# Gated linear attention as masked score blocks instead of a carried state, with a new order of the work around it

## The chip, the core and the metric

The kernel runs on one core of a Trainium2 chip. The engines named below are TensorE (PE, the matrix engine; PEld is its weight load), VectorE (DVE), ScalarE (ACT), GpSimd (POOL) and SyncE (SP, which here only starts DMAs). Each takes its own instructions in order, and they wait for each other through semaphores. The metric is the device time of one execution in microseconds (us), the median of several runs.

## What is computed

Two decoder layers over 272 tokens (16 meta tokens and 256 of the sequence), width 1024. Each layer is a half-step SwiGLU FFN, a mixer and a second FFN, each followed by a residual with ALPHA and a LayerNorm. The mixer of layer 0 is a gated short convolution. That of layer 1, which the change is about, is gated linear attention (GLA): four heads of 128 key and 256 value channels, in chunks of 64 tokens, each with a forget gate per key channel. Cut to that part:

```python
log_a = log_sigmoid(gz @ w_gate_up + b_gate) / 16.0
b = cumsum(log_a within a chunk)
scores = (q * exp(b - b_ref)) @ (k * exp(b_ref - b)).T      # within a chunk, causal
o_intra = scores @ v
o_inter = (q * exp(b)) @ state                              # state of the chunks before
state = exp(b_last) * state + (k * exp(b_last - b)).T @ v
o = (o_intra + o_inter); o = o * rsqrt(mean(o * o) + eps) * norm_w
y = o * silu(g); mix = y @ w_out
```

The sum over earlier chunks can be written with the state, or as scores against the earlier keys, each with the decay of all that lies between.

## The kernel before

**Weights.** Each weight block of 1024 x 128 is a "unit": SP loads it into one of 4 raw slots, ACT rounds it into `weights_hi` (`split_hi`, L443), DVE takes the rest into `weights_lo` (`split_lo`, L776), and PE multiplies it in three passes of eight matmuls each (`multiply`, L1240 to L1242): rounded by rounded, rounded by rest, rest by rounded. There are 8 rounded slots; a raw slot is loaded again when its `split_lo` is done.

**The stage.** The GLA stage has 25 units or tiles, j = 0 to 24: the gate's input (0), keys (1 to 4), queries (5 to 8), values (9 to 16) and output gate (17 to 24). Tiles 0 to 3 are multiplied ahead of the LayerNorm (`multiply_raw`) and unfolded by DVE. After tile 24 comes the output projection from `y`. Every engine goes through j in order, in an order written out by hand: ACT evicts tile j (`gla_tile(j)`), then rounds unit j + 8, then does the small work of that step; DVE begins step j with `split_lo` of unit j + 8.

**A head, before.** ACT makes four decay factors (`decays`), POOL multiplies keys and queries by them (`apply_decays`). PE transposes the decayed keys (`turn_k`, L1481), makes the scores within chunks (`scores`, L1488), then `outers` (L1498: keys by values, per chunk) and `outputs` (scores by values, L1511, and queries by state, L1515). DVE copies keys and scores out of PSUM (`copy_k`, `copy_scores`) and carries the state (`states`, four operations in series). POOL masks the scores (`mask_scores`). The mean square (L1524) writes 32 rows for each head, and `spread_rms` (L1534) broadcasts the reciprocal root by a product with `pick`. All these products are of plain float32. On PE, `scores(h)` stands behind tile 11 + 2h, `outers(h)` behind tile 12 + 2h and `outputs(h)` behind tile 13 + 2h.

**The end.** `gate_output` (POOL) multiplies each of eight chunks by its gate, ACT rounds it (`round_y`), DVE takes the rest (`y_low`), and the projection's product k waits for chunk k.

## Time and profile before

| | us |
|---|---|
| median of 3 runs | 1046.56 (1046.51 to 1048.36) |
| the profiled execution | 1047.89 |
| its span (first to last instruction) | 1046.2 |
| PE busy | 1032.3 (99%) |
| DVE busy | 714.5 (68%) |
| ACT busy | 512.4 (49%) |
| POOL busy | 112.4 (11%) |
| GLA stage on PE: tile 4 begins, output projection begins | 724.20, 824.42 |

The profile is of one execution, and its own time is 1.3 us above the median of the runs. Matmul durations overlap: a matmul of 272 columns is shown with 0.29 us, but the next begins 0.126 us later. So PE work is priced here by the distance between starts, which the chain of waits gives (a piece there is the time that an instruction adds). PEclk is the clock granted to TensorE as a share of 2.4 GHz.

### The profile page before, as it was taken

The page shows a single profiled execution, that of the slowest core. Times are in us where ns is not written, and L with a number is a line of the kernel's source. Part 1 is how long each engine was busy: PE and PEld are TensorE (multiplying, and loading weights), DVE is VectorE, ACT ScalarE, POOL GpSimd, SP SyncE. Part 2 cuts the span into 40 slices and gives each one's busy share as a digit, 9 for nine tenths or more (in the row PEclk, how much of TensorE's full clock was granted, in tenths as well). Part 3 has the DMA queues.
Part 4 walks back from the last instruction along what each step waited for, and adds up shares of the span by engine and source line. Part 5 has one row for each costly group of instructions (what it writes and reads, how often), then busy time and mean ns, then how long its engine had stood idle before and what let it go on. Part 6 is the DMA issues. An engine that isn't in the chain of part 4 may idle for free.

```text
span 1046.2 us, 19131 instructions
## 1 busy us (share of the span) xinstructions
PE 1032.3 (99%) x7934; PEld 1004.0 (96%) x7934; DVE 714.5 (68%) x1081; ACT 512.4 (49%) x746; POOL 112.4 (11%) x129
## 2 busy tenths in 40 slices
PE   9999999999999999999999999999899999999997
PEld 7999999999999999999999999999898999999885
DVE  5856557699789765566796555668744899756544
ACT  6533434464456434344564443546844766444440
POOL 3000002220002000013300000232121220000000
PEclk9999999999999999999999999999999999999999
DMA  9866555628653865556467655562742438865531
GB/s 258 252 182 181 166 163 177 183 80 237 201 167 106 238 181 170 158 168 186 126 197 206 174 169 162 173 172 82 203 115 86 133 110 245 233 186 183 181 122 41
DMA packets 324264, 176.60 MB, mean 169 GB/s; under 512 B 6658, under 2 KB 320048, under 8 KB 324176
## 3 DMA queue, kind: packets, MB, share of 16 engines
q1 hardware_dynamic: 323664, 174.15, 57.4%
q8 instruction: 63, 1.03, 0.4%
q0 software_dynamic: 480, 1.15, 0.4%
q14 instruction: 25, 0.20, 0.1%
q10 hardware_dynamic: 32, 0.07, 0.0%
HBM read 174.29 MB, written 1.05 MB: 168 GB/s over the span
## 4 chain that ended last, share of the span: by engine, by line
PE 93%; issue 2%; DVE 2%; ACT 1%; POOL 1%; POOLq 0%; DVEq 0%
PE bank L1240 26%; PE bank L1242 26%; PE bank L1241 26%; PE bank L1384 2%; PE bank L1386 2%; PE bank L1385 2%; PE bank L1265 2%; PE bank L1267 2%; PE bank L1266 2%; PE bank L1498 1%; PE bank L1515 1%; ACT weights_hi L443 0%; PE bank L1511 0%; DVE weights_lo L776 0%; PE bank L1524 0%
## 5 line engine op out<-in xcount | busy, mean ns | idle before, releaser
L776 DVE TENSOR_TENSOR weights_lo<-raw_weights,weights_hi 128x1024 fp32r<-128x1024 f32 x334 | 412.7, 1241 | 238.9 <-ACT weights_hi L443 237.9
L443 ACT ACTIVATE weights_hi<-raw_weights 128x1024 fp32r<-128x1024 f32 x335 | 354.2, 1060 | 424.9 <-PE bank L1242 345.2
L1240 PE MATMUL bank<-x_hi,weights_hi 128*128 128x272 f32 (+1 forms) x1632 | 471.1, 289 | 1.0 <-ACT kT L659 0.8
L1242 PE MATMUL bank<-x_hi,weights_lo 128*128 128x272 f32 (+1 forms) x1632 | 469.5, 288 | 0.0
L1241 PE MATMUL bank<-x_lo,weights_hi 128*128 128x272 f32 (+1 forms) x1632 | 467.8, 287 | 0.0
L1240 PEld LDWEIGHTS bank<-x_hi,weights_hi 128*128 128x128 f32 x1632 | 308.1, 189 | 4.8 <-issue 2.9
L1242 PEld LDWEIGHTS bank<-x_hi,weights_lo 128*128 128x128 f32 x1632 | 308.2, 189 | 0.0
L1241 PEld LDWEIGHTS bank<-x_lo,weights_hi 128*128 128x128 f32 x1632 | 308.1, 189 | 0.0
L1242 PE MATMUL bank<-mid_hi,weights_lo 128*128 128x272 f32 x528 | 152.4, 289 | 0.0
L1240 PE MATMUL bank<-mid_hi,weights_hi 128*128 128x272 f32 x528 | 152.2, 288 | 0.0
L1241 PE MATMUL bank<-mid_lo,weights_hi 128*128 128x272 f32 x528 | 151.6, 287 | 0.0
L1240 PEld LDWEIGHTS bank<-mid_hi,weights_hi 128*128 128x128 f32 x528 | 99.5, 189 | 0.0
L1241 PEld LDWEIGHTS bank<-mid_lo,weights_hi 128*128 128x128 f32 x528 | 99.5, 188 | 0.0
L1242 PEld LDWEIGHTS bank<-mid_hi,weights_lo 128*128 128x128 f32 x528 | 99.2, 188 | 0.0
L946 DVE TENSOR_TENSOR prod<-bank,silu_g 128x272 f32<-128x272 f32 (+1 forms) x82 | 35.7, 435 | 46.1 <-PE bank L1242 45.4
L368 POOL TENSOR_TENSOR total<-resid 128x272 f32<-128x272 f32 x3 | 2.7, 884 | 432.1 <-DVE resid L805 432.1
L385 POOL TENSOR_TENSOR resid<-resid,mean 128x272 f32<-128x272 f32 (+1 forms) x40 | 33.0, 862 | 142.4 <-ACT mean L480 142.4
L1265 PE MATMUL bank<-zg_hi,weights_hi 128*128 128x274 f32 (+1 forms) x160 | 47.2, 295 | 0.0
L1267 PE MATMUL bank<-zg_hi,weights_lo 128*128 128x274 f32 (+1 forms) x160 | 46.2, 289 | 0.0
L1266 PE MATMUL bank<-zg_lo,weights_hi 128*128 128x274 f32 (+1 forms) x160 | 46.0, 288 | 0.0
L952 DVE TENSOR_TENSOR mid_lo<-prod,mid_hi 128x272 fp32r<-128x272 f32 (+1 forms) x88 | 38.6, 439 | 3.0
L1384 PE MATMUL bank<-weights_hi,mid_hi 128*128 128x512 f32 x88 | 35.0, 397 | 0.0
(207 smaller groups left out, 1035.2 us busy)
## 6 DMA issues: line engine op xcount, KB each, us to landing
raw_weights<-in_ffn_w_in_dram SPq DMA_DIRECT2D x176, 512.0 KB, 4.4
raw_weights<-in_ffn_w_out_dram SPq DMA_DIRECT2D x70, 512.0 KB, 3.5
raw_weights<-in_conv_w_in_dram SPq DMA_DIRECT2D x24, 512.0 KB, 4.1
raw_weights<-in_gla_w_in_dram SPq DMA_DIRECT2D x24, 512.0 KB, 4.1
raw_weights<-in_ffn_w_out_dram SPq DMA_DIRECT2D x24, 384.0 KB, 3.2
raw_weights<-in_conv_w_out_dram SPq DMA_DIRECT2D x8, 512.0 KB, 4.6
raw_weights<-in_gla_w_out_dram SPq DMA_DIRECT2D x8, 512.0 KB, 3.6
x_tok<-in_x_dram SPq DMA_DIRECT2D x2, 512.0 KB, 4.8
```

The lines of the kernel that those rows point to most:

```text
L385: nc.gpsimd.tensor_tensor(resid[:, k, cols], resid[:, k, cols], mean[:, cols], ALU.subtract).then_inc(centred, 1)
L443: nc.scalar.activation(w_hi[:, n % RING, :], raw[:, n % RAW, :], ACT.Copy).then_inc(hi_split, 1)
L776: nc.vector.tensor_tensor(w_lo[:, s, :], raw[:, n % RAW, :], w_hi[:, s, :].bitcast(F32), ALU.subtract).then_inc(lo_split, 1)
L946: nc.vector.tensor_tensor(prod[:, s, cols], bank[2 * (t % PAIRS) + 1][:, 0:n_tok], silu_g[:, s, cols], ALU.mult).then_inc(prod_ready, 1)
L952: nc.vector.tensor_tensor(mid_lo[:, at_t, cols], prod[:, s:s + 1, cols], mid_hi[:, at_t, cols].bitcast(F32), ALU.subtract).then_inc(mid_re ...
L1240: nc.tensor.matmul(ps, w_h, hi[:, k, cols], start=first and k == k0, stop=False)
L1241: nc.tensor.matmul(ps, w_h, lo[:, k, cols], start=False, stop=False)
L1242: mm = nc.tensor.matmul(ps, w_l, hi[:, k, cols], start=False, stop=last and k == k1 - 1)
L1265: nc.tensor.matmul(ps, w_h, zg_hi[:, k, cols], start=k == 0, stop=False)
L1266: nc.tensor.matmul(ps, w_h, zg_lo[:, k, cols], start=False, stop=False)
L1267: mm = nc.tensor.matmul(ps, w_l, zg_hi[:, k, cols], start=False, stop=k == KD - 1)
L1384: nc.tensor.matmul(ps, mid_hi[:, k, toks], w_hi[:, slot, cols], start=first, stop=False)
```

## The change

It touches the GLA stage.

- **No state.** `turn_k`, `outers`, `states`, `copy_k` and `spread_rms` are gone. The 272 tokens are cut into four chunks of 64 and a rest of 16, and the keys stand in two tiles of 128 and one of 16. POOL writes keys times decay into `k_tiles`; DVE brings keys and queries further forward by whole chunks (`late_decays`: two products over 128 elements and three small steps). `scores(h)` is now seven products into one bank, of 48, 64, 144, 64, 64, 16 and 16 columns. `outputs(h)` has for each half of the values three products, of 256, 144 and 16 columns. DVE copies 400 columns and a 16 x 16 corner, POOL masks both.
- **Mean square.** POOL adds the two squares of a head (`sum_squares`), PE makes one product with a full matrix for each head, and DVE inverts each head's 256 columns (four reciprocals in place of two).
- **Full matrices.** The gate's second product has 128 rows in place of 17, and `logits` come one by one: behind tile 4, twice inside tile 5 and behind it. PSUM banks are dealt out anew: tiles 4, 5 and 6 share them in turn, logits have 0 to 3, and values turn in bank 7.
- **Order.** `outputs(h)` stands one tile earlier (behind tile 12 + 2h). PE no longer waits for the last key tiles' evictions before tiles 4 to 6. On ACT, evictions, value copies and decays stand ahead of `split_hi` in each step, and the units to be split come later (table `SPLITS`): unit 14 in step 9, 16 in step 11, 18 and 19 in step 13, 21 and 22 in step 15, 24 and 25 in step 17, from step 18 on j + 8. DVE splits first in each step, as before.
- **Residual.** ACT's eight `take_residual` of the LayerNorm ahead of the stage move from between its `x_hi` steps to steps 13 to 16, two each.
- **Last chunks.** `gate_output(6)` and `(7)` move from POOL to DVE.

DVE in the steps 10 and 11. In these rows `weights_lo` is `split_lo`, `scaled` and `d_last` are the differences for a head's decays, `gate_area` holds the running sums, `sT` the scores. Before:

```order
L776 TENSOR_TENSOR weights_lo<-raw_weights,weights_hi 128x1024 [waits hi_split] x2
L1130 TENSOR_TENSOR scaled<-gate_area 128x256 [waits exps_ready,scanned]
L1132 TENSOR_TENSOR d_last<-gate_area 128x192
L1135 TENSOR_TENSOR d_last<-gate_area 128x16
L1143 COPY k_tok<-bank 16x128 [waits k_turned]
L1143 COPY k_tok<-bank 128x128
L1143 COPY k_tok<-bank 64x128
L1150 COPY sT<-bank 128x256 [waits scores_made]
L776 TENSOR_TENSOR weights_lo<-raw_weights,weights_hi 128x1024 [waits hi_split]
L1161 COPY state<-bank 128x256 [waits exps_ready,outer_made]
```

After:

```order
L789 TENSOR_TENSOR weights_lo<-raw_weights,weights_hi 128x1024 [waits hi_split] x2
L1145 TENSOR_TENSOR d_last<-gate_area 128x256 [waits exps_ready,scanned]
L1147 TENSOR_TENSOR scaled<-gate_area 128x256
L1149 TENSOR_TENSOR scaled<-gate_area 128x16
L1160 TENSOR_TENSOR k_tiles<-k_tiles,decay 128x2x64 [waits kst_ready,exps_ready]
L1162 TENSOR_TENSOR k_tiles<-k_tiles,decay 128x2x64 [waits late_step]
L1166 COPY sq<-qT 128x64 [waits decayed]
L1167 TENSOR_SCALAR sq<-qT,decay 128x80
L1170 TENSOR_SCALAR sq<-sq,decay 128x16 [waits late_step]
L1179 COPY sT<-bank 128x400 [waits margin_set,scores_made]
L1181 COPY sT<-bank 16x16
```

The copy of the scores stood behind the two splits and the differences, and still does, but `late_decays` of the next head has come between, and `k_tok` and `state` are gone.

ACT in step 11: `prod` is the evicted value tile, `v_tok` the turned values, `silu_g` and `e_last` are decay factors. Before:

```order
L673 ACTIVATE prod<-bank 128x272 [waits v_turned,unit_used]
L443 ACTIVATE weights_hi<-raw_weights 128x1024 [waits raw_landed3,unit_used]
L716 ACTIVATE v_tok<-bank 16x128 [waits v_turned]
L717 ACTIVATE v_tok<-bank 128x2x128
L703 ACTIVATE e_last<-d_last 128x208 [waits decayed,diffs_ready]
L704 ACTIVATE silu_g<-scaled 128x256
L705 ACTIVATE silu_g<-scaled 128x256
L706 ACTIVATE silu_g<-gate_area 128x256
L707 ACTIVATE decay<-gate_area 128x4
```

After:

```order
L668 ACTIVATE prod<-bank 128x272 [waits v_turned,unit_used]
L709 ACTIVATE v_tok<-bank 16x128 [waits margin_set,v_turned]
L710 ACTIVATE v_tok<-bank 128x2x128
L695 ACTIVATE e_last<-d_last 128x256 [waits decayed,diffs_ready]
L696 ACTIVATE decay<-gate_area 128x8
L698 ACTIVATE silu_g<-scaled 128x272
L699 ACTIVATE silu_g<-scaled 128x256
L700 ACTIVATE silu_g<-gate_area 128x256
L440 ACTIVATE weights_hi<-raw_weights 128x1024 [waits raw_landed0,unit_used]
```

The rounding of a unit stood second in the step; now it stands last, behind the value copies and the five decay factors.

The diff, cut to the order and the products:

```diff
-        Y_CHUNKS = {21: (0, 1), 22: (2, 3), 23: (4, 5), 24: (6, 7)}
+        Y_CHUNKS = {19: (0, 1), 20: (2,), 21: (3,), 22: (4,), 23: (5, 6), 24: (7,)}
+        SPLITS = {9: (14,), 10: (15,), 11: (16,), 12: (17,), 13: (18, 19), 14: (20,), 15: (21, 22), 16: (23,), 17: (24, 25)}
+        SPLITS.update({j: (j + RING,) for j in range(18, GLA_TILES - 1)})
...
         def tile_bank(j):
-            return (j - 4) % 3 if j < 10 else j % 2
+            return 4 + (j - 3) % 3
...
+            def late_decays(h):
...
+                nc.vector.tensor_tensor(tiles[:, :, 1, :], tiles[:, :, 3, :], pairs(2), ALU.mult).then_inc(late_step, 1)
+                dve.wait_ge(late_step, 2 * h + 1)
+                nc.vector.tensor_tensor(tiles[:, :, 3, :], tiles[:, :, 3, :], pairs(3), ALU.mult).then_inc(late_ready, 1)
+                dve.wait_ge(decayed, 3 * h + 3)
...
-            for h in range(HEADS):
-                apply_decays(h)
-                mask_scores(h)
-            for m in range(KD):
-                gate_output(m)
+            apply_decays(0)
+            apply_decays(1)
+            mask_scores(0)
+            apply_decays(2)
+            mask_scores(1)
+            sum_squares(0)
+            apply_decays(3)
+            mask_scores(2)
+            sum_squares(1)
+            mask_scores(3)
+            sum_squares(2)
+            sum_squares(3)
+            for m in range(KD - 2):
+                gate_output(m)
...
+            for j in range(9, GLA_TILES):
+                for u in SPLITS.get(j, ()):
+                    split_lo(n0 + u)
+                if j in (9, 11):
+                    differences((j - 5) // 2)
+                if j in (11, 13, 15):
+                    late_decays((j - 9) // 2)
                 if j in (11, 13, 15, 17):
-                    copy_k((j - 11) // 2)
                     copy_scores((j - 11) // 2)
...
+                for u in SPLITS.get(j, ()):
+                    split_hi(n0 + u)
+                if j in (13, 14, 15, 16):
+                    for k in (2 * j - 26, 2 * j - 25):
+                        take_residual(FFN_NORM[2], k, T)
...
+            def outputs(h):
+
+                pe.wait_ge(scores_masked, 2 * h + 2)
                 pe.wait_ge(v_tok_ready, VT * (h + 1))
...
-                if j in (13, 15, 17, 19):
-                    outputs((j - 13) // 2)
+                if j in (12, 14, 16, 18):
+                    outputs((j - 12) // 2)
                 if j in (11, 13, 15, 17):
-                    turn_k((j - 11) // 2)
                     scores((j - 11) // 2)
```

## Rows read from the trace of the kernel before

**Rows 1.** The page, busy time and share of the span.

```profile
PE 1032.3 (99%) x7934; PEld 1004.0 (96%) x7934; DVE 714.5 (68%) x1081; ACT 512.4 (49%) x746; POOL 112.4 (11%) x129
```

**Rows 2.** Windows: stretch, length, busy PE, PEld, DVE, ACT, POOL, PEclk, DMA.

```profile
740.00:760.00 20.00, 17.09 (x124) 16.34 (x123) 17.19 (x28) 16.30 (x34) 4.61 (x5) 0.92 0.73 195
```

**Rows 3.** Waits of PE: us in total, times, longest.

```profile
PE bank L1488 <- POOL qT L405: 1.0, 1, 1.0
...
PE bank L1240 <- ACT kT L659: 0.8, 1, 0.8
PE bank L1240 <- DVE y_lo L1183: 0.6, 1, 0.6
```

**Rows 4.** Chain of waits, tiles 13 to 15: start, us added, what.

```profile
766.74 0.22 PE bank L1511 x2
766.96 0.39 PE bank L1515 x4
...
769.37 0.33 PE bank L1481 x3
769.70 0.45 PE bank L1488 x4
770.14 0.12 PE bank L1240
...
773.16 0.11 PE bank L1470
...
773.49 1.68 PE bank L1498 x8
775.17 0.98 PE bank L1524 x4
```

**Rows 5.** Chain of waits behind tile 19, one of three such groups.

```profile
806.97 0.62 PE bank L1534 x2
```

**Rows 6.** A window of 1 us in tile 12.

```profile
758.00:759.00 1.00, 1.00 (x6) 1.00 (x5) 1.00 (x6) 0.00 (x0) 0.00 (x0) 0.50 0.57 123
```

**Rows 7.** Timeline of ACT, step 14: start, us, what, idle before.

```profile
779.40 0.40 ACT L673 ACTIVATE prod<-bank 128x272 f32<-128x272 f32 x1 [4.45 <-PE bank L1242]
779.70 1.05 ACT L443 ACTIVATE weights_hi<-raw_weights 128x1024 fp32r<-128x1024 f32 x1
780.64 0.25 ACT L716 ACTIVATE v_tok<-bank 16x128 f32<-16x128 f32 x1
...
781.06 0.36 ACT L703 ACTIVATE e_last<-d_last 128x208 f32<-128x208 f32 x1
...
782.36 0.60 ACT L724 ACTIVATE gate_area<-bank 128x512 f32<-128x512 f32 x1
782.99 0.63 ACT L728 ACTIVATE o_sq<-gate_area 128x512 f32<-128x512 f32 x1
```

**Rows 8.** Timeline of ACT, a table load.

```profile
787.93 1.28 ACT L678 ACT_TABLE_LOAD   x1
```

**Rows 9.** Timeline of DVE, step 13.

```profile
767.82 1.23 DVE L776 TENSOR_TENSOR weights_lo<-raw_weights,weights_hi 128x1024 fp32r<-128x1024 f32 x1 [1.68 <-ACT weights_hi L443]
768.97 0.42 DVE L1130 TENSOR_TENSOR scaled<-gate_area 128x256 f32<-128x256 f32 x1
...
769.73 0.68 DVE L1143 COPY k_tok<-bank 16x128 f32<-16x128 f32 x3
770.34 0.40 DVE L1150 COPY sT<-bank 128x256 f32<-128x256 f32 x1
```

**Rows 10.** Timeline of POOL, heads 0 and 2.

```profile
751.41 1.14 POOL L398 TENSOR_TENSOR k_st<-kT,e_last 128x208 f32<-128x208 f32 x1 [30.33 <-ACT e_last L703]
...
755.04 0.84 POOL L405 TENSOR_TENSOR qT<-qT,silu_g 128x256 f32<-128x256 f32 x1
759.87 0.41 POOL L413 TENSOR_SCALAR_AFFINE_SELECT sT<-sT 128x256 f32<-128x256 f32 x1 [3.99 <-DVE sT L1150]
...
771.51 0.62 POOL L398 TENSOR_TENSOR k_st<-kT,e_last 128x208 f32<-128x208 f32 x1
```

More of the change, by code:

```diff
@@ L490, in normalise @@
                         early()
-                    if k >= 2:
+                    if k >= 2 and early is None:
                         take_residual(q, k - 2, n_tok)
-                for k in range(KD - 2, KD):
+                for k in range(KD - 2, KD if early is None else 0):
                     take_residual(q, k, n_tok)
@@ new lines, in _ @@
+            for j in range(1, FOLD):
+                unfolded_k(j)
+            fold_logits(0)
+            fold_logits(1)
+            softplus(0, 0)
+            split_hi(n0 + 8)
+            fold_logits(2)
+            fold_logits(3)
+            softplus(0, 1)
+            gla_tile(4)
+            split_hi(n0 + 9)
+            softplus(1, 0)
+            softplus(1, 1)
+            gla_tile(5)
+            split_hi(n0 + 10)
+            nc.scalar.activation(table_warm[:], eps[:, 0:1], ACT.Exp)
@@ L899, in normalise @@
                 x_low(KD - 1)
-                split_lo(late + RING)
+                if early is None:
+                    split_lo(late + RING)
             def out_projection(q, n0, parts, n_tok, early=None):
@@ new lines, in _ @@
+            split_lo(n0 - 1 + RING)
+            nc.vector.memset(restart[:], 1.0).then_inc(restart_set, 1)
+            dve.wait_ge(restart_set, 1)
+            nc.vector.memset(restart[:, 0:T:CH], 0.0).then_inc(restart_set, 1)
+            split_lo(n0 + 8)
+            split_lo(n0 + 9)
+            log_sigmoid(0)
+            run_sums(0)
+            differences(0)
+            split_lo(n0 + 10)
+            for h in range(1, HEADS):
+                log_sigmoid(h)
+                run_sums(h)
@@ L1455, in _, with logits @@
             main = tokens(SEQ)
-            def logits(heads):
-                pe.wait_ge(gla_evac, 1)
+            def logits(h):
+                pe.wait_ge(gla_evac, h + 1)
                 pe.wait_ge(gate_landed, 32)
-                for h in heads:
-                    nc.tensor.matmul(bank[4 + h][:, 0:T], gate_up[:, h * P:(h + 1) * P], gzT[:], start=True,
-                                     stop=True).then_inc(logits_made, 1)
+                nc.tensor.matmul(bank[h][:, 0:T], gate_up[:, h * P:(h + 1) * P], gzT[:], start=True,
+                                 stop=True).then_inc(logits_made, 1)
@@ new lines, in scores, with product @@
+                ps = bank[0]
+                tiles = k_tiles[:, h % 2, :, :, :].rearrange("p a b i -> p a (b i)")
+                def product(keys, first, queries):
+                    rows, count = keys.shape[-1], queries.shape[-1]
+                    return nc.tensor.matmul(ps[0:rows, first:first + count], keys, queries, start=True, stop=True)
+                product(tiles[:, 0, 0:2 * CH], 0, q_pos[:, h, 0:CH - META])
+                product(tiles[:, 0, CH:3 * CH], CH - META, q_pos[:, h, CH - META:P - META])
@@ L1507, in outputs @@
                 for vt in range(VT):
[L1508 to L1516 removed]
+                    v_cols, end = slice(vt * P, (vt + 1) * P), (vt + 1) * SEQ
```

433 lines of the change are left out of this document (193 added, 240 removed).

## The prediction

> **What bounds the kernel now.** I read the page's busy times first: PE is busy for 99% of the span [rows 1], so nothing is gained that does not take work or waits off PE, and nothing is lost on the other engines until PE waits for them. Next the stretch that the change touches. From 740 to 760 us PE is busy for 17.09 of 20 us, with DVE and ACT nearly as busy as PE [rows 2]: this is the one place where the small engines are late. Of the 2.9 us that PE idles there, 1.0 us is the wait of the first scores for POOL [rows 3]; the rest is two waits ahead of turned values. Two more waits belong to the stage, 0.8 us for an evicted key tile and 0.6 us for `y_lo` [rows 3]. Then the clock: in the same window the granted clock is 0.92 [rows 2], and one microsecond of it shows 0.50, the 1.2 GHz level, with PE busy throughout [rows 6]. The missing 0.08 of 20 us is 1.6 us of PE time. It followed the three idle stretches. Last, the chain of waits gives what each product adds to PE.
>
> **PE work, before.** Per head [rows 4]: transposed keys 0.33, scores 0.45, outers 1.68, mean square 0.98, and the outputs from 766.74 to 769.37, 2.63. That is 6.07 us, for four heads 24.3. The broadcasts of the root add three groups of about 0.62 [rows 5], 1.9. Sum 26.2 us.
>
> **PE work, after.** A float32 product of 128 columns adds 0.22 and two of 64 add 0.39 together [rows 4], so 0.20 is the least that I have seen for one. Outers are four products of 256 columns, 0.42 each. A product of 144 columns then lies between 0.22 and 0.42, nearest to 128; I take 0.24. Those of 48 and 16 columns are not in the trace: by columns they would be 0.15 and 0.05, but 64 costs nearly what 128 does, so I take 0.20. Scores: six at 0.20 and one at 0.24, 1.44. Outputs: twice (0.42 + 0.24 + 0.20), 1.72. Mean square: one of 256 with its switch, about 0.55. Per head 3.71, for four 14.8. Logits in four groups in place of two: I add 0.3 for the switches (between 0 and 0.6). PE work falls by 26.2 - 14.8 - 0.3 = 11.1 us. With the small products at the lower price it would be 4 us more.
>
> **Old waits.** The logits and the turned values no longer share a bank, tile 5 does not wait for a key's eviction, and the first scores follow `late_decays` with over 3 us to spare by the steps below. So 2.9 + 0.8 goes, and the slow clock behind them: 3.7 + 1.6 = 5.3 us. What comes next on ACT (four logits, the softplus, two table loads of 1.28 [rows 8], tiles 4 to 6) has at tiles 8 and 9 only 0.7 to 0.9 us in hand; a lateness there would take back up to 1 us.
>
> **The new wait.** `outputs(0)` stands one tile earlier, but what it needs is not earlier. Start from the end of tile 11 and follow the masked scores. ACT sees the tile 0.2 later (779.20 on PE, 779.40 on ACT [rows 4, 7] give that for tile 14 and its follower). Then eviction 0.30, value copies 0.42, five decay factors 1.36 (1.30 for the old five, plus 64 more elements), and only then `split_hi`, 1.05 [rows 7]: 3.35 us. DVE's `split_lo(16)` waits for it and stands ahead of the rest: 1.15, differences 0.76 [rows 9], `late_decays` of head 1. That one is not in the trace: five small steps, three of which wait for the one before; the old three copies of 128 columns took 0.61 [rows 9], so between 0.6 and 1.4, I take 1.0. Then the copies of the scores: 0.40 for 256 columns [rows 9], so 0.55 for 400 and 0.2 for the corner. The sum is 7.0. POOL's mask, 0.41 and a small one, with hand-overs 0.75 [rows 10]: 7.8 us. PE meanwhile has turned values 0.33, scores 1.44, tile 12 3.02 from 770.14 to 773.16 [rows 4], turned values 0.33: 5.2. **PE waits 2.6 us.** What the scores cost on PE hides in it.
>
> Head 1, from the end of tile 13: ACT has two `split_hi`, DVE two `split_lo` in series but no differences, so 7.8 + 1.15 - 0.76 = 8.2 against 5.2, 3.0 us. Head 2, from tile 15: no decays on ACT, 8.2 - 1.36 less a little overlap, 6.8, 1.6 us. Head 3: ACT comes from `copy_o(2)` and its square, 1.26 [rows 7], then table load and root (1.28 + 0.6 [rows 8]), `split_hi`, two residuals (0.8), another table load, tile 17, values, two `split_hi`: some 9.2 us from the end of `outputs(2)`; then DVE 1.15 + 1.15 and copies, mask: 12.0. PE has in this time mean square, tiles 17 and 18, values, scores, 8.2. 3.8 us. **Sum of the new waits 11.0 us.** Queued behind PE's wait are all later tiles; DVE and ACT have spare time then. The eight residuals (3.3 us of ACT) move into this chain, but only two of them (0.8) lie on its path, and they give 0.2 us at tile 4.
>
> **The end.** DVE gets four reciprocals and scales, done some 4 us before the projection, and gates 6 and 7. By the same steps `y_lo(7)` is nearly in time: of the wait of 0.6 nothing to 0.6 stays; I take 0.6 as gained. Nulls: the reset of `gate_up` and the dropped `pick` lie in the start, with POOL idle.
>
> **The sum.** -11.1 - 5.3 + 11.0 - 0.6 = -6.0 us. New idle can lower the clock again. Idle of 2.9 us in three pieces cost 1.6 us before; now there are three pieces of 2.6 to 3.8 us. I count one drop, +1.6. So -4.4: 1047.9 becomes 1043.5 by the profiled execution, which is 1.3 above the median; **1042.1 us** in the runs.
>
> The Trainium skill, TensorE: Matmul & The Clock Gate, section "HAM oscillation — how this bites in real kernels", says that a matmul stream with waits between its pieces falls back to the slow clock again and again. The trace agrees so far with its one drop. By that rule all three long waits would be paid for, 4.8 us, and the time would be 1045.3.
>
> **Rivals.** (A) *The waits are much smaller.* If DVE and ACT run ahead of my steps (short small operations, less in series), up to none of the 11 us and no slow clock stay: 1046.6 - 17.0 = 1029.6; with half of them 1035. For it: PE alone is sure to lose 11 us of work. Against: the order of ACT and DVE is fixed, and the long steps have rows. 0.27 for 1029 to 1039.
> (B) *No difference.* Each of the four chains is 0.7 longer (`late_decays` at 1.4, margins at tiles 8 and 9 lost) and the clock falls three times: -6.0 + 2.8 + 4.8 = +1.6, 1048. 0.13 for 1044.5 to 1048.7.
> (C) *Slower: POOL and DVE hold each other up.* POOL's four products for head 0 lasted from 751.41 to 755.9; the first alone took 1.14 beside DVE's splits and 0.62 later [rows 10]. The next `decays` on ACT wait for POOL, and `split_hi` now stands behind them, so POOL's lateness reaches every engine. At 1.5 us per head and four clock drops: -6.0 + 6.0 + 6.4 = +6.4, 1053. It decides once POOL's five products take over 4.5 us in every head. POOL is idle in three of the four chains, which speaks against it. 0.10.
> The Trainium skill, SBUF — State Buffer, section "Who interferes with whom", says that a DVE instruction with two SBUF inputs and a GpSimd instruction that reads SBUF exclude each other, the second waiting for the first to end. The 1.14 against 0.62 agrees. By it the rival (C) is real wherever the two meet.
> (D) That the change doesn't do what it says is excluded by the order of the instructions.
>
> **Chances.** Forecast, 1039 to 1044.5: 0.50; A 0.27; B 0.13; C 0.10. A measurement of this kernel tells 0.2%, 2.1 us, from no change. Faster 0.77, same 0.13, slower 0.10. A range of 1031 to 1046 leaves out some 0.05 below and 0.15 above.
>
> **What would show it.** PE's waits for the mask (POOL `sT`) ahead of `outputs`, of 2.6, 3.0, 1.6 and 3.8 us; DVE's `split_lo` waiting for ACT just ahead of them; the PE stretch from tile 4 to the projection down from 100.2 to about 94 us; turned keys, outers and broadcasts gone, and 3.7 us per head in their place; the granted clock below 1 once. Wrong would be: no waits for POOL (then A), waits early at tiles 7 to 9, or scores of 7 products well off 1.44 us.

## Result and the profile after

The changed kernel takes **1053.19 us** (median of 5, 1051.36 to 1055.61) beside 1046.92 us for the kernel before on the same chip: a ratio of 1.0054, 95% interval 1.0038 to 1.0069. It is slower by half a per cent, where 1042.1 was forecast with a range of 1031 to 1046. The profiled execution took 1053.19 us, its span is 1051.4 us. Granted clock, mean over the span:

```profile
core 0: 1051.4 us, clock 0.991
```

PE's waits of over 0.2 us (line of the waiting instruction, who released it; total, times, longest):

```profile
PE bank L1541 <- POOL sT L402: 8.7, 4, 3.6
PE bank L1506 <- ACT v_tok L710: 3.5, 1, 3.5
PE bank L1279 <- DVE y_lo L1205: 3.0, 2, 2.3
PE bank L1406 <- DVE idle L1029: 2.0, 1, 2.0
```

L1406 is the start and was there before. All the waits of [rows 3] ahead of the projection are gone. In their place stand 8.7 us for the mask (L1541, `outputs`), 3.5 us at a turned value (L1506, `turn_v(1)`) and 3.0 us for `y_lo`, which was 0.6.

What PE does for one head answers to [rows 4]. PE's timeline behind tile 16 and behind tile 17 (start, duration with overlap, what):

```profile
790.21 0.70 PE L1541 MATMUL bank<-sT,v_tok 128*128 128x256 f32 x2 [1.24 <-POOL sT L402]
790.74 0.41 PE L1543 MATMUL bank<-sT,v_tok 128*128 128x144 f32 x2
790.99 0.29 PE L1545 MATMUL bank<-sT,v_tok 128*128 128x16 f32 x2
791.13 0.68 PE L1541 MATMUL bank<-sT,v_tok 128*128 128x256 f32 x2
...
792.03 0.68 PE L1552 MATMUL bank<-o_sum,meanV 128*128 128x256 f32 x2
792.36 0.47 PE L1279 MATMUL bank<-x_hi,weights_hi 128*128 128x256 f32 x1
```

```profile
795.71 0.56 PE L1523 MATMUL bank<-q_pos,k_tiles 128*128 128x48 f32 x4
796.10 0.46 PE L1523 MATMUL bank<-sq,k_tiles 128*128 128x144 f32 x2
...
797.07 0.21 PE L1523 MATMUL bank<-q_pos,kT 128*16 128x16 f32 x2
797.21 0.39 PE L1279 MATMUL bank<-x_hi,weights_hi 128*128 128x256 f32 x1
```

By the starts the outputs take 1.82 us (790.21 to 792.03), the mean square 0.33, the scores 1.50 (795.71 to 797.21): 3.65 us per head, in place of 6.07. (The second product of the tile that follows comes 0.30 us after its first behind a mean square and 0.23 behind scores, where 0.12 is usual; with that the head adds 3.9 us.)

Below are windows of 2 us of PE: stretch, length, busy time (instructions), granted clock as a share of 2.4 GHz, DMA share, GB/s. Before there was one stretch at 0.50 [rows 6], after there are four.

```profile
758.00:760.00 2.00, 2.00 (x11) 0.50 0.92 250
762.00:764.00 2.00, 0.79 (x5) 1.00 0.86 250
...
778.00:780.00 2.00, 2.00 (x9) 0.50 0.16 44
790.00:792.00 2.00, 1.79 (x12) 1.00 0.99 260
...
806.00:808.00 2.00, 2.00 (x9) 0.50 0.25 73
832.00:834.00 2.00, 2.00 (x12) 0.50 0.14 39
```

Each follows idle of PE: 3.5 us ending at 755.4, 2.6 at 776.5, 3.6 at 803.9, 2.3 and 0.6 at 829.8 and 831.4. After the two waits of 1.2 us (ending at 763.5 and 790.2) the clock stayed at 1.0. Summed over windows of 20 us from 700 to 840, the missing clock is worth 7.0 us of PE time, against 1.6 before: 1.7 us for each stretch.

**Where the span's 5.2 us come from.** Three measures serve all kernels below. S is the start of the first product with `total`, which ends FFN 0; F is the time from the second to the fourth of these, two FFNs that the change does not touch; L is that from the fourth to the fifth, which holds the gated attention and its projection. Before: S 212.5, F 401.6, L 138.0. After: 213.3, 402.8, 141.0. So L gives +3.0, F +1.2, S +0.8. L adds up as: PE's work -12.4 (four heads at 3.65 for 26.2, and the logits, which in four groups cost 0.8 less than in two), old waits -3.7, mask +8.7, turned value +3.5, `y_lo` +2.4, clock +5.4. That is +3.9, 0.9 too much. The balance can be drawn without these terms: over just the stretch that L measures, PE was idle for 4.4 us before and 15.1 after, the slow clock took 1.7 and 6.8, and what is left is its work at full clock, 131.9 and 119.0 (windows of 1 us, summed). So work -12.9, idle +10.7, clock +5.1: +2.9, which is L within its rounding.

### The profile page after: what moved, and what is told of

It is laid out like the page before. It is cut to its first block, busy times and chain, and to the rows that moved or that the text cites. A ratio compares the mean times of both kernels' runs of the same rounds, so it can differ in the third digit from the quotient of the medians.

```text
span 1051.4 us, 18995 instructions
## 1 busy us (share of the span) xinstructions
PE 1026.4 (98%) x7866; PEld 1004.6 (96%) x7866; DVE 716.5 (68%) x1084; ACT 512.3 (49%) x745; POOL 115.1 (11%) x130
## 4 chain that ended last, share of the span: by engine, by line
PE 88%; issue 5%; DVE 3%; POOL 2%; ACT 1%; DMA 1%; SPq 0%; POOLq 0%; DVEq 0%; ACTq 0%
PE bank L1281 25%; PE bank L1279 25%; PE bank L1280 25%; PE bank L1423 2%; PE bank L1425 2%; PE bank L1424 2%; PE bank L1306 2%; PE bank L1305 2%; PE bank L1304 2%; DMA raw_weights<-in_ffn_w_in_dram 1%; ACT weights_hi L440 1%; DVE resid L905 0%; DVE x_lo L892 0%; POOL q_pos L411 0%; DVE rms L1186 0%
```

## The experiments

All times are medians; the ratio is to the kernel before on the same chip. "Clock" is the time that the lowered clock is worth between 700 and 840 us, in the profiled execution.

| kernel | us | ratio, 95% interval | S | F | L | clock |
|---|---|---|---|---|---|---|
| before | 1046.9 | 1 | 212.5 | 401.6 | 138.0 | 1.6 |
| after | 1053.2 | 1.0054 [1.0038, 1.0069] | 213.3 | 402.8 | 141.0 | 7.0 |
| a1_places | 1051.7 | 1.0031 [1.0015, 1.0046] | 215.2 | 401.5 | 139.3 | 7.0 |
| b1_places | 1048.6 | 1.0010 [0.9999, 1.0021] | 216.0 | 402.8 | 136.6 | 1.8 |
| a2_copy_first | 1043.4 | 0.9954 [0.9936, 0.9972] | 213.0 | 402.9 | 128.1 | 3.4 |
| a3_fill | 1050.7 | 1.0035 [1.0022, 1.0048] | 213.4 | 402.8 | 138.1 | 5.2 |
| a4_margins | 1036.3 | 0.9896 [0.9878, 0.9913] | 213.3 | 402.8 | 124.0 | 1.8 |
| a5_end | 1037.4 | 0.9898 [0.9881, 0.9914] | 215.9 | 402.8 | 126.5 | 1.8 |
| a6_all | 1035.4 | 0.9883 [0.9865, 0.9901] | 215.2 | 401.5 | 125.2 | 1.8 |
| a7_outputs_later | 1048.7 | 1.0003 [0.9988, 1.0019] | 216.0 | 402.9 | 136.7 | 10.2 |
| a8_end2 | 1039.4 | 0.9920 [0.9907, 0.9933] | 213.8 | 402.8 | 127.2 | 3.4 |
| a9_all2 | 1037.6 | 0.9908 [0.9889, 0.9926] | 215.2 | 401.5 | 127.6 | 3.4 |
| a10_residual_back | 1038.9 | 0.9914 [0.9900, 0.9927] | 213.5 | 402.9 | 126.8 | 1.8 |
| a11_margins_only | 1055.9 | 1.0079 [1.0066, 1.0092] | 216.0 | 402.9 | 141.4 | 6.8 |
| a12_lnexp | 1033.6 | 0.9864 [0.9844, 0.9884] | 216.0 | 402.8 | 120.2 | 0 |
| a13_end3 | 1032.9 | 0.9862 [0.9847, 0.9876] | 213.0 | 402.9 | 120.8 | 0 |
| a14_lnexp_places | 1032.1 | 0.9857 [0.9835, 0.9879] | 212.6 | 401.5 | 120.5 | 0 |
| a15_best | 1034.0 | 0.9861 [0.9839, 0.9883] | 215.2 | 401.5 | 121.1 | 0 |
| a16_end_only | 1050.0 | 1.0024 [1.0010, 1.0037] | 213.2 | 402.9 | 139.0 | 8.6 |

S scatters by 3.5 us between profiles. With the old places of the buffers (before and the kernels with the edit of a1_places) it is 212.5 and 212.6, or 215.2; with the new ones 213.0 to 213.8, or 215.9 and 216.0. Which of the two groups, over 2 us apart, a profile falls into goes with nothing that was edited, and a few executions of one kernel scatter as much (a2: 1040.0 to 1044.7). F scatters by 0.1 and tells edits apart best. L does not hold so still: a1_places and b1_places have the same instructions in this stretch as after and before, and their L is 1.7 and 1.4 us shorter, mainly because one wait of PE is missing in each (1.2 us for the first mask, 0.9 for a turned value). So a difference in L of under 2 us shows nothing by itself. S, F, L and the clock are each of one execution, and not always of a middling one: that of a2_copy_first was the fastest of its 6 and that of a7_outputs_later 3.1 us above its median.

### The places in SBUF: a1_places, b1_places

```diff
         scaled = sb("scaled", [P, 3, T])
+        gzT = sb("gzT", [P, T])
+        gate_up = sb("gate_up", [P, DK])
+        pad = sb("pad", [P, 32])
         silu_g = sb("silu_g", [P, SETS, T])
...
-        gzT = sb("gzT", [P, T])
-        gate_up = sb("gate_up", [P, DK])
```

b1_places: the kernel before without the line `h_f = sb("h_f", [P, 3, T])`.

> The changed kernel with nothing but the places of buffers in SBUF changed: gzT, gate_up and 32 unused columns stand where the unused h_f stood before, so that silu_g, prod and the FFN's mid_hi and mid_lo lie again at the addresses of the kernel before. Theory 1 (the 1.9 us that are missing before tile 4 come from the places of mid_hi and mid_lo): the FFN output products come back from 127 to 125 ns apart, tile 4 begins near 724.2 us and the time falls by about 1.8 us, to some 1051.4. Rival (the early part is slower for another cause, such as the moved residual scaling or the cleared gate_up): tile 4 stays at 726 us and the time within 0.5 us of 1053.2.

> The kernel before with nothing but the unused buffer h_f taken out, so that silu_g and everything behind it lies 3264 bytes lower, as in the changed kernel. Theory 1 (places): the time rises by 1.8 us to about 1048.7, with tile 4 at about 726 us and the output products of the FFNs 127 ns apart in place of 125. Rival: no change, 1046.9 within 0.5 us.

F is 401.5 with the old places and 402.8 with the new, in both kernels, and so in every later pair. The groups of instructions by form show which products: those that read `mid_hi` and `mid_lo` (busy us, mean ns; the pass over `mid_lo` stands for the three). First before, then after, then a1_places, then b1_places:

```profile
L1241 PE MATMUL bank<-mid_lo,weights_hi 128*128 128x272 f32 x528 | 151.6, 287 | 0.0
```

```profile
L1280 PE MATMUL bank<-mid_lo,weights_hi 128*128 128x272 f32 x528 | 152.9, 290 | 0.0
```

```profile
L1281 PE MATMUL bank<-mid_lo,weights_hi 128*128 128x272 f32 x528 | 151.6, 287 | 0.0
```

```profile
L1240 PE MATMUL bank<-mid_lo,weights_hi 128*128 128x272 f32 x528 | 152.9, 290 | 0.0
```

Theory 1 holds in the traces: 0.65 us per FFN, from an unused buffer that was taken out. The first FFN lies in S, and within either group of S the old places are the earlier ones (by 0.4 us or more in the first, 0.7 to 0.8 in the second), so three FFNs come to near 2 us. The medians alone would not show it: b1_places is 0.9 us above the kernel before on its chip (1048.6 and 1047.6, where +1.8 was expected), with an interval that contains no change, and the intervals of a1_places and of after overlap. Tile 4 did not begin at 724.2 in a1_places, since S was 1.9 later in that profile. Which property of the addresses does it no run tells.

### The order of the copies on DVE: a2_copy_first, a7_outputs_later

The chain of the first mask in after, on ACT (rounding of a unit), DVE (rest of that unit, copy of the scores) and POOL (mask):

```profile
758.18 1.04 ACT L440 ACTIVATE weights_hi<-raw_weights 128x1024 fp32r<-128x1024 f32 x1
```

```profile
759.25 1.23 DVE L789 TENSOR_TENSOR weights_lo<-raw_weights,weights_hi 128x1024 fp32r<-128x1024 f32 x1 [1.63 <-ACT weights_hi L440]
...
762.22 0.57 DVE L1179 COPY sT<-bank 128x400 f32<-128x400 f32 x1
```

```profile
762.93 0.41 POOL L399 TENSOR_SCALAR_AFFINE_SELECT sT<-sT 128x256 f32<-128x256 f32 x1 [10.05 <-DVE sT L1181]
```

DVE stands idle for 1.6 us until ACT has rounded, and only then come the rest of the unit, the differences, `late_decays(1)` and the copy. PE starts the outputs at 763.5.

```diff
             for j in range(9, GLA_TILES):
+                if j in (11, 13, 15, 17):
+                    copy_scores((j - 11) // 2)
+                if j in (11, 13, 15):
+                    late_decays((j - 9) // 2)
                 for u in SPLITS.get(j, ()):
                     split_lo(n0 + u)
                 if j in (9, 11):
                     differences((j - 5) // 2)
-                if j in (11, 13, 15):
-                    late_decays((j - 9) // 2)
-                if j in (11, 13, 15, 17):
-                    copy_scores((j - 11) // 2)
```

> The changed kernel with one order changed on DVE: in the steps of tiles 11, 13, 15 and 17 the copies of the scores stand first, then late_decays of the next head, and only then the roundings (split_lo) that wait for ACT. Theory 2 (the copies and the mask are late because a rounding that waits for ACT is queued ahead of them): PE's waits for the mask, 1.2, 2.6, 1.2 and 3.6 us, fall to nothing to 0.5 us each, since copies 0.63 and mask 0.75 are less than the 3.0 us of the tile that PE has in between. -8.7 us, and one to two clock drops less (-1.6 to -3.2): 1041 to 1044. Rival 2a (the roundings become late in turn and PE waits for lo_split one or two tiles on): the sum of waits falls by under 4 us, 1049 or more. Rival 2b (POOL comes late at the mask, since it is at the next head's decays): waits of 1 us or more stay at heads 0 to 2.

PE's waits in a2_copy_first:

```profile
PE bank L1506 <- ACT v_tok L710: 3.5, 1, 3.5
PE bank L1279 <- DVE y_lo L1205: 3.2, 3, 2.3
```

No wait for `sT` is left, and L falls by 12.9 us: 8.7 of waits, 3.6 of clock. Theory 2 holds, 2a and 2b fall. The edit takes the copies out from behind the roundings, the differences and `late_decays` at once; which share each of these has was not measured apart. a7_outputs_later gives PE more cover instead and leaves DVE's order alone:

```diff
-                if j in (12, 14, 16, 18):
+                if j in (13, 15, 17, 18):
                     outputs((j - 12) // 2)
...
-                if j in (14, 16, 18, 20):
+                if j in (15, 17, 19, 20):
                     mean_square((j - 14) // 2)
```

(`copy_o` and `root_ms` on ACT move with them.)

> The changed kernel with its own order on DVE, but the outputs of heads 0 to 2 (with their copies, squares and mean squares) one tile later, as in the kernel before; those of head 3 stay after tile 18. Theory 2 (the mask's chain is about 7 to 8 us and PE has only one tile, 5 us, to cover it): with a second tile of 3 us and more the waits for the mask of heads 0 to 2 (1.2, 2.6 and 1.2 us) go, that of head 3 stays at 3 to 4.5 us; one or two clock drops go too: -5.0 - 1.6 to -3.2, that is 1045 to 1047. Rival (the waits are for POOL as such, which is busy with the decays): the waits stay, 1052 or more.

The waits of heads 0 to 2 went, that of head 3 was 2.9 us. But the time was 1.7 us above the top of what I gave: in the profiled execution the clock was worth 10.2 us, 3.2 more than after. By windows of 4 us its three slow stretches (from 756, 796 and 824 us) are worth 3.4 us each, the four of after 1.7 each. Fewer waits did not mean less slow clock there. That execution is one of the slower ones, though: the twelve lie between 1044.8 and 1053.1, and the four with a granted clock of 0.992 or 0.993 over the span took 1044.8 to 1047.3, about as expected, the eight with 0.988 to 0.990 took 1048.2 or more.

### Filling the waits: a3_fill

```diff
+                if h:
+                    pe.wait_ge(o_copied, h)
+                for _ in range((9, 21, 9, 29)[h]):
+                    nc.tensor.matmul(bank[3][:, 0:T], minus128[:], z0_hi[:], start=True, stop=True)
                 pe.wait_ge(scores_masked, 2 * h + 2)
                 pe.wait_ge(v_tok_ready, VT * (h + 1))
-                if h:
-                    pe.wait_ge(o_copied, h)
```

(The wait for `o_copied` only moves ahead of the added products, which write the bank that it guards.)

> The changed kernel with unneeded products ahead of the four waits for the mask: 9, 21, 9 and 29 products of 272 columns of fp32r on constants, into bank 3, which the outputs overwrite. At 0.127 us each they fill about as much as PE waited there (1.2, 2.6, 1.2, 3.6 us). Nothing else is changed, so the chain that makes the mask is the same. Theory 3 (the two stretches at the slow clock, about 777 to 781 and 805 to 808 us, follow the idle of these waits): they vanish, the granted clock of these stretches is 1.0, and the time falls by 3.2 us to about 1050 although PE does 8.6 us more of work. Rival (the clock falls for another cause, or the idle costs nothing): the time stays at 1053.2 or rises.

The clock of a3_fill where after had shown 0.50, and at tile 12, ahead of which nothing was filled:

```profile
756.00:758.00 2.00, 2.00 (x12) 0.52 1.01 276
758.00:760.00 2.00, 2.00 (x10) 0.50 0.98 274
776.00:780.00 4.00, 4.00 (x30) 1.00 0.87 249
...
804.00:808.00 4.00, 4.00 (x32) 1.00 0.52 150
```

The two stretches behind the filled waits are gone, those behind unfilled ones stay. PE does 8.7 us of useless work and the kernel is 2.5 us faster. Theory 3 holds, and one profile is not all that speaks for it: head 3's wait of 3.6 us was left unfilled in after, a1_places, a11_margins_only and a16_end_only, and a slow stretch followed it in all four. The two stretches were worth 1.7 us each, 3.4 together; the stretch behind the first, unfilled wait was worth 3.4 in place of 1.7 here, and PE came to the first mask 1.4 us later, so L falls by 2.9.

### The margins: a4_margins, a11_margins_only

In after, ACT's `copy_v(0)` waits 3.4 us for a clearing of `v_tok`, which is on DVE behind `late_decays(0)` and a rounding. ACT's timeline, then DVE's, then POOL's:

```profile
754.75 0.27 ACT L709 ACTIVATE v_tok<-bank 16x128 f32<-16x128 f32 x1 [3.41 <-DVE v_tok L1231]
```

```profile
749.65 0.83 DVE L1160 TENSOR_TENSOR k_tiles<-k_tiles,decay 128x128 f32<-128x128 f32 x1
...
751.16 0.21 DVE L1166 COPY sq<-qT 128x64 f32<-128x64 f32 x1
...
752.11 0.80 DVE L1170 TENSOR_SCALAR sq<-sq,decay 128x16 f32<-128x16 f32 x1
...
754.17 0.48 DVE L1231 MEMSET v_tok<- 128x512 f32 x1
...
761.15 0.28 DVE L1160 TENSOR_TENSOR k_tiles<-k_tiles,decay 128x128 f32<-128x128 f32 x1
...
761.68 0.19 DVE L1166 COPY sq<-qT 128x64 f32<-128x64 f32 x1
...
762.07 0.23 DVE L1170 TENSOR_SCALAR sq<-sq,decay 128x16 f32<-128x16 f32 x1
```

```profile
745.59 1.21 POOL L380 TENSOR_TENSOR kT<-kT,silu_g 128x16 f32<-128x16 f32 x1
...
764.81 0.21 POOL L380 TENSOR_TENSOR kT<-kT,silu_g 128x16 f32<-128x16 f32 x1
```

`late_decays(0)` takes 3.2 us beside POOL's products, `late_decays(1)` 1.1 alone (0.83 against 0.28, 0.80 against 0.23 per step), and a POOL product of 16 columns 1.21 against 0.21. The copy with one input took 0.21 there and 0.19 alone. The edit:

```diff
+            pool.wait_ge(unit_used, unit0["gla"] + FOLD)
+            nc.gpsimd.memset(sT[:, :, 0, 0:META], 0.0).then_inc(margin_set, 1)
+            nc.gpsimd.memset(sT[:, :, 1, P + REST:P + 2 * REST], 0.0).then_inc(margin_set, 1)
+            nc.gpsimd.memset(v_tok[:, :, 2, :], 0.0).then_inc(margin_set, 1)
             apply_decays(0)
```

(and the same three away from DVE; a4_margins has the order of a2_copy_first, a11_margins_only that of the changed kernel.)

> The order of a2_copy_first, and the three clearings of the margins of sT and v_tok moved from DVE, where they stand behind late_decays(0) and two roundings, to POOL ahead of its first decays, where POOL is idle. Theory 4 (PE's wait of 3.5 us at the second turned value is a wait for these clearings, through ACT's copy_v(0)): that wait goes, and the clock drop behind it too (tile 12 took 4.6 us, three microseconds is its full-speed time). By the trace of a2_copy_first the copies of the first scores are then next, some 1 us late because DVE is busy without a gap from 738 to 757 us: -3.5 - 1.5 + 1.1, about -4 us against a2_copy_first, 1039. Rival (the wait passes whole to the next dependence, since DVE as such is the bound of this stretch): 1043 as before, with 3 us of waits at the first scores or the first mask.

> The changed kernel with its own order of copies and roundings on DVE, and only the clearings of the margins moved to POOL. Theory 4: the 3.5 us at the second turned value and most of the slow clock behind it (1.4 us) go, the waits for the mask of heads 1 to 3 stay at 2.6, 1.2 and 3.6 us, that of head 0 grows by up to 2 us because PE arrives there 4 us earlier while DVE gains only 0.7: 1049 to 1050.5, which is what separates the two causes (this one 3 to 4 us, the order of the copies 8 to 10). Rival (DVE as such is the bound there): 1052 or more, with all 3.5 us at the first mask.

PE's waits in a4_margins, then in a11_margins_only:

```profile
PE bank L1279 <- DVE y_lo L1209: 3.0, 3, 2.3
...
PE bank L1541 <- POOL sT L402: 0.7, 1, 0.7
```

```profile
PE bank L1541 <- POOL sT L402: 12.5, 4, 5.0
PE bank L1279 <- DVE y_lo L1209: 2.9, 2, 2.3
```

In a4_margins it went as expected, -4.1 us in L, with 0.7 left for the first mask. In a11_margins_only the rival came true in its place and size: the wait at the turned value went and the wait for the first mask grew from 1.2 to 5.0 us. Counted from tile 4 the first mask came after 37.4 us in after and 36.5 here. DVE is busy without a gap until 759.6, then stands 1.3 us until ACT has rounded, as in after, and the copy comes behind that. With the copies first, as in a4_margins, 0.7 us of the 12.5 of waits for masks is left: it is the copies' place on DVE that sets the mask, and the wait at the turned value only stood ahead of it. Nothing was gained (L 141.4 for 141.0; the medians' intervals overlap): in after the slow clock that followed the 3.5 us lay in tile 12, ahead of the wait for the mask, and cost nothing, since it only shortened that wait; here the slow stretch lies behind that wait. From the first mask to the second it was 13.0 us in after and 14.6 here. a1_places and a16_end_only show the same from the other side: their first slow stretch is worth 3.4 us, and the wait of 1.2 us for the first mask is gone.

### The end: a5_end, a8_end2, a12_lnexp, a13_end3, a16_end_only

In after the chunks of y come late. DVE's timeline (reciprocals of heads 2 and 3, and the roundings of y), then POOL's gates:

```profile
817.16 1.23 DVE L789 TENSOR_TENSOR weights_lo<-raw_weights,weights_hi 128x1024 fp32r<-128x1024 f32 x1 [2.94 <-ACT weights_hi L440]
...
818.63 1.75 DVE L1186 RECIPROCAL rms<-rms 128x256 f32<-128x256 f32 x1
...
829.36 0.76 DVE L1205 TENSOR_TENSOR y_lo<-q_pos,y_hi 128x256 fp32r<-128x256 f32 x2 [1.06 <-ACT y_hi L734]
...
830.93 0.43 DVE L1205 TENSOR_TENSOR y_lo<-q_pos,y_hi 128x256 fp32r<-128x256 f32 x1 [0.48 <-ACT y_hi L734]
```

```profile
821.04 0.86 POOL L411 TENSOR_TENSOR q_pos<-gate_area 128x256 f32<-128x256 f32 x1 [5.53 <-DVE gate_area L1193]
825.52 3.35 POOL L411 TENSOR_TENSOR q_pos<-gate_area 128x256 f32<-128x256 f32 x1 [3.62 <-DVE y_lo L1205]
```

Gate 5 takes 3.35 us on POOL, beside DVE's roundings, where gate 4 took 0.86. All variants but a16_end_only start from a4_margins.

> a4_margins with the end of the stage taken up: the last mean square one tile earlier (after tile 19), so root, reciprocals and scaling of heads 2 and 3 start about 2.7 us earlier; gate 5 on DVE like 6 and 7 (on POOL the last gate took 3.35 us beside DVE); the chunks of y as (2,3), 4, 5, 6, 7 in steps 20 to 24. Theory 5 (the waits of 2.9 to 3.2 us for y_lo come from the late reciprocals and from the gate that POOL makes under DVE's load): the waits for y_lo fall to under 0.6 us and the slow clock in the first chunks of the projection goes: -2.6 - 1.6 = -4.2 us against a4_margins, about 1035. Rival (the mean square itself now waits, since ACT's square and POOL's sum take until after tile 19): a wait of 0.5 to 1.5 us at it, 1036 to 1037.

a5_end: theory 5 fails in the form that I gave it. The waits for `y_lo` fell to 1.7 us, but ACT stood 5.7 us with a rounding in front of the eviction of tile 22, and PE 3.5 us behind that. ACT's timeline in a5_end:

```profile
810.89 0.42 ACT L738 ACTIVATE y_hi<-q_pos 128x256 fp32r<-128x256 f32 x1 [5.69 <-POOL q_pos L411]
811.22 0.37 ACT L677 ACTIVATE gate_area<-bank 128x256 f32<-128x256 f32 x1
```

> a4_margins with another end than a5_end had. There ACT stood with y's rounding in the step of tile 21 for 5.7 us behind a gate on POOL, and with it the eviction of tile 22, for which PE waited 3.5 us. Here gates 4 to 7 are all on DVE, each one step ahead of its rounding on ACT; the reciprocal and scaling of heads 0, 1, 2, 3 stand singly in DVE's steps 16, 17, 19 and 20 in place of two pairs in 17 and 20; the last mean square comes after tile 19. Theory 5 (DVE, with 7.0 us of reciprocals and 3.5 of scalings, sets when y is complete; they must start earlier, not just the root): the scaling of head 3 ends 3 us earlier by the trace of a4_margins, y_lo(7) about 811 us in place of 815, so the waits for y_lo fall from 3.0 to under 1 us and the slow clock there (1.4 us) goes: about -3.5 us, 1032.5 to 1033. Rival (head 0's reciprocal, 2.6 us of DVE with its scaling, delays the copies of head 3's scores): a wait of 1 to 2 us for the mask of head 3 takes half of it back, 1034.5.

a8_end2: the rival in kind, and more than it in size. Head 0's reciprocal in step 16 stands ahead of the copies of head 3's scores, and the wait for the mask of head 3 was 3.3 us, where 1 to 2 were given; a slow stretch of 3.4 us followed it. The waits for `y_lo` fell to 1.2 us, but the time is 3.1 us above a4_margins and 4.9 above what the rival named. a12_lnexp and a13_end3 leave head 0 in step 17. The end of a13_end3:

```diff
-        Y_CHUNKS = {19: (0, 1), 20: (2,), 21: (3,), 22: (4,), 23: (5, 6), 24: (7,)}
+        Y_CHUNKS = {19: (0, 1), 20: (2,), 21: (3,), 22: (4,), 23: (5,), 24: (6, 7)}
...
-                if j == 17:
-                    for h in range(2):
-                        invert_rms(h)
-                        scale_o(h)
-                if j == 23:
-                    gate_output(KD - 2)
+                if j == 22:
+                    gate_output(5)
                 if j == 24:
-                    gate_output(KD - 1)
+                    gate_output(7)
                 for m in Y_CHUNKS.get(j, ()):
                     y_low(m)
-                if j == 20:
-                    for h in range(2, HEADS):
-                        invert_rms(h)
-                        scale_o(h)
+                if j in (21, 23):
+                    gate_output(j - 17)
+                for h in {17: (0, 1), 19: (2,), 20: (3,)}.get(j, ()):
+                    invert_rms(h)
+                    scale_o(h)
```

(POOL keeps gates 0 to 3; the last mean square and its root come after tile 19. a12_lnexp makes the inverse root of heads 2 and 3 on ACT with two operations, Ln and Exp, in place of root and reciprocals.)

> a4_margins with the inverse root of heads 2 and 3 made on ACT, as Exp(-0.5 Ln(x + eps)) after tile 19, in place of a root there and two reciprocals of 1.75 us on DVE; gates 4 to 7 on DVE, each ahead of its rounding. Heads 0 and 1 stay as they are. Theory 5 (DVE's queue at the end is the cause of the waits for y_lo): DVE has 3.5 us less, the scaling of heads 2 and 3 ends near 801 us in place of 807.4, the waits for y_lo fall from 3.0 to under 0.5 us and the slow clock behind them (1.4 us) goes: -4 us against a4_margins' 1036.2, 1032. Rival (ACT becomes the bound: two more table loads of 1.28 and 0.7 of work at tile 19 delay evictions and roundings): waits of 1 to 3 us for ACT at tiles 22 to 24, 1034 to 1036.

> a4_margins with the order of the end as in a12_lnexp, but root on ACT and reciprocals on DVE as before (heads 0 and 1 in step 17, head 2 in 19, head 3 in 20). If the gate on POOL (3.35 us under DVE's load) and not DVE's queue was the cause of the late y_lo, the waits fall from 3.0 to under 1 us, 1033. If DVE's queue is the cause, they stay at 2 to 3 us and the time at 1036.

> The changed kernel with only its end as in a13_end3: gates 4 to 7 on DVE each ahead of its rounding, the last mean square and root after tile 19, head 2's reciprocal in step 19 and head 3's in step 20. If the end's term stands by itself, the waits for y_lo fall from 3.0 to about 1.2 us and the slow clock in the first chunk goes (1.6): -3.4 us, 1049.8. Rival: with the mask of head 3 late (3.6 us) the chunks of y are as late as before, since copies, mask and square of head 3 all come after it: waits for y_lo stay over 2 us, 1052 or more.

PE's waits in a13_end3:

```profile
PE bank L1276 <- DVE y_lo L1209: 1.2, 2, 0.6
PE bank L1538 <- POOL sT L402: 0.7, 1, 0.7
```

Both bring L down by over 3 us (1.8 of it clock) and the clock in this stretch to 1.0 throughout. a13_end3, with all its reciprocals on DVE, is as fast as a12_lnexp, so they need not leave DVE. Which part of the edit does it is not shown: gates 4 and 5 left POOL, and the reciprocals of heads 2 and 3 began 3.1 and 1.6 us earlier (799.1 and 803.2 for 802.2 and 804.8 in a4_margins), together. Alone on the changed kernel (a16_end_only) the edit is worth 3.2 us by the medians, as expected (1050.0 for 1049.8), 2.0 in L: the waits for `y_lo` fell from 3.0 to 1.1 us and the slow stretch behind them went, but two others were worth 3.4 us each, and the clock took 8.6 us in all.

### The moved residual, and the best kernel: a10_residual_back, a6_all, a9_all2, a14_lnexp_places, a15_best

a10_residual_back is a8_end2 with `take_residual` of the last norm at its old place on ACT.

> a8_end2 with the residual's scaling of the last norm ahead of the gated attention back at its old place, behind the roundings of x in the norm, and out of ACT's steps of tiles 13 to 16. The prediction priced its move at 0.2 us gained at tile 4 and 0.8 us on the mask's chain. With the copies first on DVE, ACT has room there, so only the 0.2 us should be seen: the same time as a8_end2 within 0.5 us. Rival (its eight operations delay x_hi and the first evictions of the stage): PE waits at tiles 4 to 6, 1 us or more.

L 126.8 against 127.2: the move of the residual brings nothing that can be measured. (The profiles differ in two ways that nearly cancel: 1.8 for 3.4 us of slow clock, and a wait of 0.5 us for a key tile that a8_end2 has not. The rest is within the scatter of L.) The other four put the edit of a1_places on a5_end, a8_end2, a12_lnexp and a13_end3.

> a5_end with the places in SBUF of a1_places. If the effect of places adds up with the rest, 1.3 to 2 us less than a5_end, near 1033; if it was an accident of the executions, the same as a5_end. The FFN output products should come 125 ns apart, not 127.

> a8_end2 with the places in SBUF of a1_places. FFN output products 125 ns apart; 1.3 to 2 us less than a8_end2, near 1031.

> a12_lnexp at the places of a1_places: the FFN output products 125 ns apart, 1.3 to 2 us less than a12_lnexp, near 1030.5.

> a13_end3 at the places of a1_places. Between the fourth and the fifth mean_total product 120.8 us as in a13_end3 (120.5 by a14_lnexp_places), between the second and the fourth 401.5 in place of 402.9: 1 to 2 us less than a13_end3 (1032.9), 1031 to 1032.

F falls by 1.3 or 1.4 in all four. In the medians it shows in three (-2.0, -1.7, -1.5) and not in a15_best, 1.1 above a13_end3, with S 2.2 later. All four times came out above those expected: a6_all and a9_all2 by 2.4 and 6.6 us, since a5_end and a8_end2 under them had, a14_lnexp_places by 1.6 and a15_best by 2. a12 to a15 cannot be told apart by their ratios, 0.9857 to 0.9864. They take 1.4% less than the kernel before and some 20 us less than the changed one.

## Why the prediction was wrong

- **PE work, -11.1: right, 1.3 to 1.8 too small.** Measured -12.4 by the pieces, -12.9 by the balance. Scores 1.50 for 1.44, outputs 1.82 for 1.72, mean square 0.33, with its switch 0.5, for 0.55. The logits in four groups saved 0.8 where I added 0.3.
- **Old waits and their clock, -5.3: right.** All gone.
- **The waits for the mask, +11.0: right in mechanism and place, a little too large.** 1.2, 2.6, 1.2 and 3.6 us for 2.6, 3.0, 1.6 and 3.8. The step that I priced without a row, `late_decays`, took 1.1 where I took 1.0. a2_copy_first shows that what was queued ahead of the copies was the cause.
- **"At tiles 8 and 9 only 0.7 to 0.9 us in hand; a lateness there would take back up to 1 us": this step failed.** It cost 3.5 us at `turn_v(1)`. I followed ACT's evictions and left out that the change gives `copy_v` a wait of its own, for clearings on DVE. DVE was at the end of a stretch without a gap, and POOL's products stretched its steps to three times their length. That is the mechanism of rival C, while C was priced over every head. a11_margins_only shows that DVE and not this one wait bounds the stretch.
- **One clock drop, +1.6: this step failed the most.** Four drops, 7.0 us. I had 11 us of idle in four pieces in the sum and counted one drop for it, although [rows 6] showed one for 2.9 us. a3_fill shows that the idle is the cause and that two of the drops cost 3.4 us together. The Trainium skill, TensorE: Matmul & The Clock Gate, section "HAM oscillation — how this bites in real kernels", has the return to the slow clock paid for again behind each wait between bursts of matmuls; the trace agrees for the four waits of over 2 us, and a1_places has one of 2.6 us that was not paid for. By that rule the prediction named 1045.3, with which rival B would have been the forecast.
- **The end, -0.6: wrong sign.** Measured +2.4 of waits and its share of the clock. "By the same steps `y_lo(7)` is nearly in time" was not worked out: gates 4 and 5 stayed on POOL, which under DVE's load takes 3.35 us for one (the one before it took 0.86), and the late reciprocals stand ahead of them; the runs do not part the two. a16_end_only prices the term at 3.2 us.
- **Nulls.** "The reset of `gate_up` and the dropped `pick` lie in the start" holds, but the dropped `h_f` was not looked at, since nothing reads it. It moved every buffer behind it by 3264 bytes: +1.3 us in F, near +2 with the first FFN.
- **Residual: 0.2 gained.** Nothing to be seen in the time.

The sum with what was measured: work -12.9, idle +10.7, clock +5.1 = +2.9, and +2 for the places, of the 5.2 us of the span. From the forecast's -4.4 that is 9.6 us away: the clock +5.1, the turned value +3.5, the end +3.0 and the places +2.0, less 2.3 for the smaller waits for the mask and 1.8 for the work. Rival C gave the time, 1053. Its four clock drops came true (7.0 us for 6.4), but its 6.0 us of contention in every head did not: POOL's five products took 5.1 us for head 0, then 3.6 and 3.1 for the next two, where C wanted over 4.5 in every head. That the turned value, the end and the places, less the smaller masks and the work, came to 4.4 us in its stead was luck.

## What to carry to other kernels

On an in-order engine, put what the bound engine waits for ahead of the work that waits for a third engine: the same instructions in another order were worth 10 us of 1050. Price a forecast's idle twice, as wait and as slow clock. Only what lies behind the last wait of a chain counts: as a11_margins_only shows, a slow stretch ahead of a wait that it only shortens is free, and a wait taken away ahead of a later one can gain nothing. Follow every semaphore that a change adds to an old step back to the engine that raises it, and to all that is queued there.

## What the hardware showed unexpectedly

- Moving buffers by 3264 bytes changes products of 272 columns on `mid_hi` and `mid_lo`, with the same instructions. Over the three passes of one FFN their starts are 125.5 ns apart in before and 126.9 in after, 124.5 and 126.9 in the pass over `mid_lo`. Two FFNs take 401.5 or 401.6 us against 402.8 or 402.9 in all 19 kernels, none between.
- Useless products in a wait made the kernel 2.5 us faster.
- A slow stretch is worth either 1.7 us or 3.4, nothing between, in the GLA stage and its projection in all 19 profiles. Neither the length of the wait ahead nor the instructions settle which: the wait of 3.5 us at the turned value is followed by 1.7 in after and by 3.4 in a1_places, which has the same instructions, and the later wait of 2.6 us by 1.7 in after and by nothing in a1_places. Of the 28 waits of 2.3 to 5.0 us there, 25 had a slow stretch right behind them; a single wait of 0.8 us had one too, in b1_places. What sets it no run tells, and for a forecast it means a chance and not a fixed price.
- A DVE step with a scalar column, 16 columns wide, took 0.80 us beside a POOL product and 0.23 alone, a copy with one input 0.21 and 0.19. The Trainium skill, SBUF — State Buffer, section "Who interferes with whom", counts `tensor_scalar` among the steps that can take the ports that DVE shares with GpSimd; the trace agrees. It counts copies too; this one was not held up.
- The start scatters: the first `total` product came at 213.0 to 213.8 or at 215.9 to 216.0 us in kernels whose starts hold the same instructions at the same places. No run tells why.
